# Half a forward transform, and evictions behind the fourth half unit

## The reference

```
# first block
z_u, z_v, z_h, z_g = split(h @ w_in + b_in)          # 1024, 1024, 3*1024, 2*2048 columns
y_b = hyena(z_h) @ w_branch_b
  # hyena: y = v; for gate in (x1, x2):
  #   y = gate * (irfft(rfft(y, 512) * k_spec, 512)[:256] + y * skip)
mix = (sigmoid(z_ga) * y_a + sigmoid(z_gb) * y_b) @ w_o + b_o
x = layer_norm(ALPHA * x + g1 * mix)
# second block, pooling mixer
z = xn @ w_in; u, g = split(z)
mixed = einsum('bsgc,gcd->bsgd', pooled(u), w_group) # 4 groups of 1024 x 1024
out = (mixed * scale * silu(g)) @ w_out
```

## Time and profile before

| | us |
|---|---|
| median of 3 runs | 2732.11 |
| lowest and highest | 2728.93, 2734.42 |
| the profiled execution | 2727.24 |
| its span | 2725.9 |

### The profile page before, as it was taken

One profiled execution on the slowest core, in us unless ns is written; L12 is line 12 of the kernel. 1 busy time (PEld: TensorE's weight loads), 2 busy tenths in 40 slices (PEclk: granted clock), 3 DMA queues, 4 the chain that ended last, 5 costly groups with the idle time before them and its releaser, 6 DMA issues.

```text
span 2725.9 us, 31673 instructions
## 1 busy us (share of the span) xinstructions
PE 2645.5 (97%) x12574; PEld 2195.6 (81%) x12574; DVE 1846.9 (68%) x1933; ACT 1281.7 (47%) x1552; POOL 35.9 (1%) x58
## 2 busy tenths in 40 slices
PE   4899999999999999999999899999999999999999
PEld 2569998888878888888888788788888888888887
DVE  6878877877896654577666867755554565556565
ACT  2234444334344444555555444444444565555463
POOL 0000000000000000000000000000000000000000
PEclk8899999999999999999999999999999999999999
DMA  9988778878868865565656555555566555633654
GB/s 322 344 302 280 265 259 281 285 268 312 301 227 300 278 216 186 185 207 194 199 187 200 178 187 186 170 182 184 183 209 199 180 190 163 193 116 129 211 185 139
DMA packets 268965, 598.45 MB, mean 220 GB/s; under 512 B 12739, under 2 KB 13390, under 8 KB 258398
## 3 DMA queue, kind: packets, MB, share of 16 engines
q1 hardware_dynamic: 259680, 561.56, 60.8%
q0 software_dynamic: 5232, 25.23, 2.7%
q10 hardware_dynamic: 3918, 9.79, 1.0%
HBM read 586.05 MB, written 10.49 MB: 219 GB/s over the span
## 4 chain that ended last, share of the span: by engine, by line
PE 90%; DVE 6%; DMA 2%; issue 1%; ACT 1%; SPq 0%; DVEq 0%; ACTq 0%
PE ps L830 26%; PE ps L832 26%; PE ps L831 26%; PE ps L930 2%; PE ps L917 2%; PE ps L916 2%; PE ps L914 2%; DVE w_lo L2036 1%; DVE group_acc L2170 1%; DMA raw<-in_w_ada 1%; DMA raw<-in_w_in 1%; PE ps L997 0%; PE ps L1012 0%; PE ps L1004 0%; PE ps L1323 0%
## 5 line engine op out<-in xcount | busy, mean ns | idle before, releaser
L2036 DVE TENSOR_TENSOR w_lo<-raw,w_hi 128x1024 fp32r<-128x1024 f32 x870 | 1049.2, 1221 | 687.4 <-ACT w_hi L1424 685.6
L1424 ACT CAST w_hi<-raw 128x1024 fp32r<-128x1024 f32 x870 | 906.8, 1051 | 1072.5 <-PE ps L832 954.0
L830 PE MATMUL ps<-w_lo,x_hi 128*128 128x512 f32 x2592 | 1017.9, 393 | 8.8 <-DVE w_lo L2036 4.9
L832 PE MATMUL ps<-w_hi,x_lo 128*128 128x512 f32 x2592 | 1010.6, 390 | 0.0
L831 PE MATMUL ps<-w_hi,x_hi 128*128 128x512 f32 x2592 | 1010.0, 390 | 0.0
L830 PEld LDWEIGHTS ps<-w_lo,x_hi 128*128 128x128 f32 x2592 | 487.5, 188 | 112.5 <-issue 7.3
L832 PEld LDWEIGHTS ps<-w_hi,x_lo 128*128 128x128 f32 x2592 | 487.3, 188 | 102.5
L831 PEld LDWEIGHTS ps<-w_hi,x_hi 128*128 128x128 f32 x2592 | 487.5, 188 | 99.7 <-issue 0.7
L830 PE MATMUL ps<-w_lo,pooled_hi 128*128 128x512 f32 x384 | 152.0, 396 | 6.8 <-DVE w_lo L2036 6.8
L2064 DVE SCALAR_TENSOR_TENSOR ada_acc<-raw,cond,ada_acc 128x2048 f32<-128x2048 f32 x64 | 150.0, 2344 | 0.3 <-DMA raw<-in_w_ada 0.3
L831 PE MATMUL ps<-w_hi,pooled_hi 128*128 128x512 f32 x384 | 150.2, 391 | 0.0
(11 more groups left out here) (377 smaller groups left out, 2195.6 us busy)
## 6 DMA issues: line engine op xcount, KB each, us to landing
raw<-in_w_m SPq DMA_DIRECT2D x128, 1024.0 KB, 5.2
raw<-in_w_in SPq DMA_DIRECT2D x72, 1024.0 KB, 5.8
raw<-in_w_ada SPq DMA_DIRECT2D x64, 1024.0 KB, 5.0
raw<-in_pool_w_in SPq DMA_DIRECT2D x64, 1024.0 KB, 5.3
raw<-in_w_ada SPq DMA_DIRECT2D x64, 512.0 KB, 5.9
raw<-in_pool_w_out SPq DMA_DIRECT2D x32, 1024.0 KB, 5.0
raw<-in_ple_w_gate SPq DMA_DIRECT2D x32, 1024.0 KB, 5.1
raw<-in_mla_w_in SPq DMA_DIRECT2D x24, 1024.0 KB, 5.1
```

What stands on the lines that cost most here:

```text
L830: mm(bank, xh, wl, start=start, stop=False)
L832: ins = mm(bank, xl, wh, start=False, stop=stop)
L1424: nc.scalar.copy(by_ktile(st, w_hi[st.half_slot(j, half)][:, 0:n]), raw_half(st, j, half)).then_inc(hi_split, 1)
L2036: tt(by_ktile(st, w_lo[slot][:, 0:n]), raw_half(st, j, half), by_ktile(st, w_hi[slot][:, 0:n].bitcast(F32)), ALU.subtract).then_inc(lo_spl ...
```

## The change

The forward transform is done on 128 frequencies instead of 256. Tokens are put in the order even, odd, and frequencies in the order f, 255-f. For the frequency 255-f the cosines of even tokens are those of f and those of odd tokens are negated (for the sines the other way round), so the sums over even tokens E and over odd tokens O give both: re is E+O and E-O, im is E+O and O-E. `forward` makes E and O apart in four banks of `ps`, ACT copies the two O banks out (`hy_odd`), and DVE forms the sums in `even_and_odd`, four instructions of 128 x 512, two of them written to `ps`. `multiply` is cut into `multiply_re` and `multiply_im`. The three pieces come before half units 12, 13 and 14, `signal_rest` before half unit 8 and now behind two "a" blocks, `yb_rest(0)` before half unit 15. ACT's `round_products` waits for both products. `turn_signal` reads every second token.

In `mix` and in the group product chunks of `pool_g` the hook comes after the fourth half unit instead of the second. In `w_o`, `o_prepare` moves from the hook to the chunk's tail (`o_prepare(c)` behind chunk c's last load), and a weight unit comes before the first "a" block of the rest. `pool_g_hook` gets two waits of DVE on `product_ready`, which DVE itself counts up.

```diff
-    ("in_vu", 1, [("ww", "awwa")] * 2), ("in_h", 2, A2), ("in_h2", 1, A2), ("in_g", 4, A2),
-    ("mix", 1, [("w", "wa")] * 8), ("w_o", 1, [("ww", "awwa")] * 4),
+    ("in_vu", 1, [("ww", "awwa")] * 2), ("in_h", 2, A2), ("in_h2", 1, A2), ("in_g", 4, [("wwa", "wwaa"), ("ww", "wwa")]),
+    ("mix", 1, [("ww", "a")] * 8), ("w_o", 1, [("ww", "wawa")] * 4),
-    ("pool_u", 4, W2), ("pool_g", 4, [("w", "w"), ("ww", "ww")] * 2), ("pool_out", 4, [("ww", "wwwwww")]),
+    ("pool_u", 4, W2), ("pool_g", 4, [("ww", ""), ("ww", "ww")] * 2), ("pool_out", 4, [("ww", "wwwwww")]),
...
 # turn_signal
-  nc.tensor.transpose(ps[:, 6 + t, ct * P:(ct + 1) * P], hy[b][:, 0, ct, t * P:(t + 1) * P], ident[:])
+  nc.tensor.transpose(ps[:, 6 + t, ct * P:(ct + 1) * P], hy[b][:, 0, ct, t:S:2], ident[:])
 # forward
             for m in range(2):
-                for f in range(2):
-                    part = slice(f * P, (f + 1) * P)
-                    for t in range(2):
-                        bank = ps[:, 4 + 2 * m + f, :]
-                        mm(bank, dft_hi[:, m, t, part], hy_lo[:, t, :], start=t == 0, stop=False)
-                        mm(bank, dft_hi[:, m, t, part], hy_hi[:, t, :], start=False, stop=False)
-                        ins = mm(bank, dft_lo[:, m, t, part], hy_hi[:, t, :], start=False, stop=t == 1)
+                for t in range(2):
+                    bank = ps[:, 4 + 2 * m + t, :]
+                    mm(bank, dft_hi[:, m, t, 0:P], hy_lo[:, t, :], start=True, stop=False)
+                    mm(bank, dft_hi[:, m, t, 0:P], hy_hi[:, t, :], start=False, stop=False)
+                    ins = mm(bank, dft_lo[:, m, t, 0:P], hy_hi[:, t, :], start=False, stop=True)
 # ACT, in_g, ahead of gate(n - 1)
+                if c:
+                    act.wait_ge(hy_f, i + 1)
+                    nc.scalar.copy(hy_odd[:], ps[:, 5:8:2, :]).then_inc(odd_copied, 1)
 # ACT, round_products
-                act.wait_ge(hy_prod, 2 * n + m + 1)
+                act.wait_ge(hy_prod, 2 * n + 2)
 # DVE
+        def even_and_odd(n):
+            dve.wait_ge(odd_copied, n + 1)
+            dve.wait_ge(hy_f, n + 1)
+            odd = hy_odd[:]
+            tt(hy_re[:, 0], ps[:, 4, :], odd[:, 0], ALU.add)
+            then(tt(hy_re[:, 1], ps[:, 4, :], odd[:, 0], ALU.subtract))
+            tt(ps[:, 4, :], ps[:, 6, :], odd[:, 1], ALU.add)
+            then(tt(ps[:, 5, :], odd[:, 1], ps[:, 6, :], ALU.subtract))
...
-            run(st, i, in_g, lambda i, n: (3, 4 * i + n), tail=lambda i, c: products_rest(i) if c else signal_rest(i))
+            run_at(st, i, {4: lambda: in_g(i, 0), 8: lambda: signal_rest(i), 12: lambda: in_g(i, 1),
+                           13: lambda: multiply_re(i), 14: lambda: multiply_im(i),
+                           15: lambda: yb_rest(0) if i == 2 else None, 16: lambda: products_rest(i)},
+                   lambda i, n: (3, 4 * i + n))
 # w_o
             else:
-                o_prepare(c - 1)
                 branch_add(0, ST["w_o"], c - 1)
         def w_o_tail(i, c):
             if c == 0:
                 mixed_rest(3)
-            if c == 3:
-                o_prepare(3)
+            o_prepare(c)
```

More of the change, by code:

```diff
@@ L54, in tables @@
     cos_tf, sin_tf = np.cos(t * w), np.sin(t * w)
-    dft = np.stack([cos_tf, -sin_tf, (cos_tf / S).T, (-sin_tf / S).T])
+    tokens = np.concatenate([np.arange(0, S, 2), np.arange(1, S, 2)])
+    freqs = np.concatenate([np.arange(P), S - 1 - np.arange(P)])
+    forward = [tab[tokens][:, freqs] for tab in (cos_tf, -sin_tf)]
+    dft = np.stack(forward + [tab.T[freqs] / S for tab in (cos_tf, -sin_tf)])
     bands = (EMB - 1) // 2
@@ L59, in tables @@
     band = np.linspace(1e-4, bands - 1, bands)[None, :]
-    feats = np.concatenate([lin, np.cos(band * omega), -np.sin(band * omega)], axis=1).T
+    feats = np.concatenate([lin, np.cos(band * omega), -np.sin(band * omega)], axis=1).T[:, tokens]
     deltas = np.abs(np.linspace(math.log(1e-2) / 1.5, math.log(1e-2) / 0.3, W1))[None, :]
-    window = np.exp(-lin * deltas)
+    window = np.exp(-lin * deltas)[tokens]
     pool = np.stack([1.0 / np.minimum(np.arange(16) + 1, width) for width in WINDOWS])
@@ L222, in block_kernel @@
     hy_tmp = at("hy_tmp", 76, [2, CH])
+    hy_re = at("hy_re", 180, [2, CH])
+    hy_odd = at("hy_odd", 76, [2, CH])
     prod_hi = [at("prod_hi0", 180, [2, CH], F32R), at("prod_hi1", 136, [2, CH], F32R)]
@@ L405, in block_kernel @@
     hy_f = sem("hy_f")
+    odd_copied = sem("odd_copied")
     hy_prod = sem("hy_prod")
@@ L1065, in turn_signal @@
                 for ct in range(4):
-                    ins = nc.tensor.transpose(ps[:, 6 + t, ct * P:(ct + 1) * P], hy[b][:, 0, ct, t * P:(t + 1) * P],
-                                              ident[:])
+                    ins = nc.tensor.transpose(ps[:, 6 + t, ct * P:(ct + 1) * P], hy[b][:, 0, ct, t:S:2], ident[:])
             ins.then_inc(tm_full, 1)
@@ L1566, in round_dft @@
             act.wait_ge(fm_lo, 4)
-            nc.scalar.copy(dft_hi[:, m:m + 2], dft[:, m:m + 2]).then_inc(dft_round, 1)
+            part = slice(0, S if m else P)
+            nc.scalar.copy(dft_hi[:, m:m + 2, :, part], dft[:, m:m + 2, :, part]).then_inc(dft_round, 1)
         run_at(ST["in_vu"], 0, {2: lambda: gelu(0), 6: lambda: gelu(1), 8: lambda: round_dft(0), 10: lambda: round_dft(2),
@@ L2255, in split_dft @@
             dve.wait_ge(dft_round, m // 2 + 1)
-            tt(dft_lo[:, m:m + 2], dft[:, m:m + 2], dft_hi[:, m:m + 2].bitcast(F32), ALU.subtract).then_inc(dft_split, 1)
+            part = slice(0, S if m else P)
+            tt(dft_lo[:, m:m + 2, :, part], dft[:, m:m + 2, :, part], dft_hi[:, m:m + 2, :, part].bitcast(F32),
+               ALU.subtract).then_inc(dft_split, 1)
         run_at(ST["in_vu"], 0, {0: lambda: vu_out(0), 4: lambda: vu_out(1), 10: lambda: split_dft(0),
@@ L2301, in _, with multiply_re @@
         run(ST["in_h2"], 0, in_h2, lambda i, n: (2, 12 + n))
-        def multiply(n):
+        def even_and_odd(n):
+            dve.wait_ge(odd_copied, n + 1)
             dve.wait_ge(hy_f, n + 1)
+            odd = hy_odd[:]
[3 more added lines that the diff above has]
+            then(tt(ps[:, 5, :], odd[:, 1], ps[:, 6, :], ALU.subtract))
+        def multiply_re(n):
             dve.wait_ge(spec_in, 16 * (n + 1))
-            re, im = ps[:, 4:6, :], ps[:, 6:8, :]
+            re, im = hy_re[:], ps[:, 4:6, :]
             k_re, k_im = spec[:, 0:2], spec[:, 2:4]
@@ L2311, in multiply, with multiply_im @@
             tt(prod_re[:], prod_re[:], hy_tmp[:], ALU.subtract).then_inc(hy_prod, 1)
+        def multiply_im(n):
+            re, im = hy_re[:], ps[:, 4:6, :]
+            k_re, k_im = spec[:, 0:2], spec[:, 2:4]
             dve.wait_ge(hy_prod, 2 * n + 1)
@@ L2367, in in_g @@
             if n % 2:
-                multiply(n // 2)
+                even_and_odd(i)
             elif n:
-                regate(n // 2 - 1)
-            if n == 5:
-                yb_rest(0)
+                regate(i - 1)
         st = ST["in_g"]
         for i in range(4):
-            run(st, i, in_g, lambda i, n: (3, 4 * i + n), tail=lambda i, c: products_rest(i) if c else signal_rest(i))
+            run_at(st, i, {4: lambda: in_g(i, 0), 8: lambda: signal_rest(i), 12: lambda: in_g(i, 1),
+                           13: lambda: multiply_re(i), 14: lambda: multiply_im(i),
+                           15: lambda: yb_rest(0) if i == 2 else None, 16: lambda: products_rest(i)},
+                   lambda i, n: (3, 4 * i + n))
         st = ST["mix"]
@@ L2721, in pool_g_hook @@
                     dve.wait_ge(fm_full, 44)
+                else:
+                    dve.wait_ge(product_ready, 2 * i)
                 copy_pair(st, i, 0, 0, group_out[:])
@@ L2734, in pool_g_hook @@
             if c == 3:
+                dve.wait_ge(product_ready, 2 * i + 1)
                 copy_pair(st, i, 2, 0, group_out[:])
```

## The result

| | before | after |
|---|---|---|
| median, 4 runs each | 2730.52 | 2705.6 |
| lowest to highest | 2728.38 to 2734.42 | 2702.92 to 2708.09 |
| the profiled execution | 2727.24 | 2702.92 |
| its span | 2725.9 | 2701.5 |

The ratio is 0.991, 95% interval 0.9899 to 0.9922: 24.9 us faster. The forecast was 24.8 us, and 2707.3. That time was reckoned from a median before of 2732.1 in three runs; with the fourth it is 2730.5.

The account below looks back on a forecast made before the run. PE was taken to bound the kernel, busy 97% and carrying 90% of the chain. Terms 10.4 + 1.3 + 2.6 + 0.6 + 9.9 = 24.8 us took the median 2732.1 to 2707.3, range 2701 to 2718, chance 0.72.

Parts of the forecast that it names:

- Forward: Forward transform in `in_g`: 48 fewer matmuls save 10.9 us of PE, less a 0.5 stall, net 10.4.
- The third round's stall: In `in_g`'s third round, `yb_round` and `yb_rest` make the inverse ready at 24.9 for 24.5; PE stands about 0.5 us.
- Price of writing to `ps`: DVE's sums in the transform: 0.71 us each, as the 512-wide row; upper bound a 1024 row, 1.22, about 4.5 in all.
- Rival 1: In `in_g` DVE decides, its sequence of products coming too late for PE: 2712 to 2718 us, chance 0.12.
- Waits on DVE's own instruction: Six waits in the transform's DVE sequence cost about 0.11 us each, 0.7 in all; without them no third-round stall, 0.5 lower.
- Mix: In `mix`, the hook behind the fourth half unit removes PE's 1.02 us wait; gain 1.3 with restart.
- w_o: In `w_o`, three PE waits, 1.8 us together, vanish before half unit five; gain 2.6 with 0.27 restart each.
- End of w_o: At the end of `w_o`, DVE's last eviction starts earlier after PE's last product; gain about 0.6 us toward the norm.
- pool_g: In `pool_g`, eight PE waits, 6.8 us together, go except one near 0.5; with the clock behind the longest, gain 9.9.
- Transposes: In `turn_signal`, reading every second token costs nothing, as 8 bytes apart is near to dense; upper bound 3.5 to 4.5 us.
- Rival 3: The strided transposes cost time as each weight load doubles: 2711.5 us, chance 0.05.
- Rivals 2 and 4: 2: `mix` and `pool_g` stalls move one chunk, 2714.5 us, chance 0.06; 4: `mix` and `w_o` loads late, 2741, chance 0.03.

Follow-up runs that it names:

- e1: The changed kernel's transform and `in_g` order, with `mix`, `w_o` and `pool_g` ordered as in the kernel before; median 2718.56 us, ratio 0.9965.
- e3: The changed kernel with the even and odd sums and both products in one piece before half unit 12, instead of three pieces; median 2710.16 us, ratio 0.9934.
- e5: The changed kernel with four more 512-wide DVE sums ahead of the four of each transform; 2707.21 us in one profiled execution.
- e4: The changed kernel with ACT's table loaded early, `yb_round(0)` and `yb_rest(0)` one round later, and `ff_prepare(3)` and `x2_out` moved; median 2700.43 us, ratio 0.9893.
- e6: The kernel before with only `o_prepare` moved from the hook to the chunk's tail in `w_o`; 2730.73 us in one profiled execution, `w_o` 88.06.

## Why the prediction was right

- **Forward, 10.4 forecast, 10.11 measured.** 48 matmuls of 0.227 are gone, and an undisturbed round is 53.03. The third round's stall came near the forecast: PE is 0.36 late and the round 53.49, 0.46 more. The 0.3 that is missing is the 0.1 by which each of three rounds shrank less than 2.72, mostly in the transposes. e1 gives the same 10.10 alone. The chain of e3 and e5 shows the margin that the forecast leaned on: 1.6 us at half unit 14.
- **Price of writing to `ps`.** Taken as the 512-wide row, measured 0.68 to 0.70. Rival 1 lived on the upper bound; e5 shows what it would have cost, 5.3 us for 2.4 of work a round, near the 4.5 that was forecast.
- **Waits on DVE's own instruction, 0.11 each.** Of the rows above, 453.46 to 454.59 is 1.13 without such a wait and 454.59 to 455.85 is 1.26 with it; 512 wide it is 0.61 (449.44 to 450.05) and 0.71 (450.05 to 450.76). The Trainium skill, VectorE: DVE Perf Modes, section The DRAIN you can't avoid, says that such a semaphore costs nothing extra. These distances say otherwise. The third round's stall does not decide it, though the forecast tied it to the rule. Six waits were counted there, 0.7 in all; three cost something, in the sums and in each product (in the second round before 450.76, 455.85 and 460.51), since the others come behind a split or a wait for ACT. In the third round DVE stands 0.84 for ACT at 505.93, which swallows the first of the three. Without the other two, 0.24, PE would still be about 0.1 late (an estimate from the 0.36). What makes the stall is `yb_round` and `yb_rest`: e4 takes them out of that round and gets 0.47 back.
- **Mix 1.3 (1.31), w_o 2.6 (2.73).** By the rows of single waits the restart is 0.29 in `mix` and 0.30 for each of three in `w_o`, near the 0.27 that was taken. e6 corrects the reason in `w_o`: moving `o_prepare` is enough.
- **End of w_o, 0.6 forecast, nothing measured.** This is the term that failed. I followed DVE's chain of eviction, statistics, norm, and did not look at the chain beside it, PE's 32 small matmuls of 3.6 us and `mod`. Before, DVE's chain was already the earlier one: it waited 0.17 for PE. So a faster eviction could bring nothing, however fast.
- **pool_g, 9.9 forecast, 10.20 measured.** Seven waits gone, and the clock's loss behind the longest; the new chain to the 0.47 came true link by link. By the starts of the half units the longest cost 4.39 (forecast 4.4), the seven others 6.58 (6.2) and the one that is left 0.76 (0.65). The 0.3 more lie in the seven: their restart is 0.32 each and not 0.27. e4 confirms the table load as the one link that counts there.
- **Transposes.** The forecast says that it is wrong if their weight loads pass 200 ns. They do, 209, so by its own sign it was wrong here, and so was its reason that 8 bytes apart is near to dense. The term of nothing should have been 0.3 us: the loads are 32 x 69 ns = 2.2 us longer in all, and all but 0.3 of it lies beside PE's matmuls. The sign asked for the load's duration, where only what PE's matmuls lose counts. That so little shows on PE was not reasoned ahead, and that is luck. Rival 3 multiplied loads by their growth (3.5 to 4.5 us), which is far too much.
- **Rivals 2 and 4.** No wait moved to the next chunk's first half unit except where forecast. No load came late at the changed slots: x had 4.7 us to spare in `w_o` and PE does not wait in either stage. By how much the weight loads could have been slower was not tried.
- The sum by stages is 10.11 + 1.31 + 2.73 - 0.12 + 10.20 = 24.2 for 24.8 forecast. The misses are -0.3, 0, +0.1, -0.7 and +0.3, and in part they cancel. The two spans differ by 24.4. The 24.9 of the medians hold the runs' scatter, so that agreement to 0.1 us is luck.

## What to carry to other kernels

Where one engine prepares tiles for another in turn, write down for each tile when it is wanted and when it is ready; the smallest difference is the room for other work there, and a share of busy time says nothing of it. Long work goes in pieces with a tile between them, so that at each tile all the work ahead of it still ends before the tile is wanted. Before counting a gain in a chain that ends in a join, look at which branch ends last: shortening the earlier one brings nothing, and shortening the later one brings at most the distance to the other.

## What the runs showed of the hardware

Weight loads of 128x128 f32 from the state buffer took 140 ns at a step of 1 element, 209 at 2, 212 at 4 and 187 at 8. An instruction of DVE that waits for its own predecessor starts later than one that does not: 0.71 for 0.61 us from start to start with 512 elements, 1.26 for 1.13 with 1024. Both were mostly hidden here, the first behind PE's matmuls but for 0.3 us, the second in DVE's spare time but for one round.
